# Tokens as the stationary side in the value projections and the second feed-forward product, x turned to rows once, last norm and store row by row

## The reference

```python
def memory_attention(q, mem_n, w_mk, w_mv):
    k = (mem_n @ w_mk).reshape(b_, -1, MEM_HEADS, MEM_HEAD_DIM)
    v = (mem_n @ w_mv).reshape(b_, -1, MEM_HEADS, MEM_HEAD_DIM)
    ...
# second block: 8 retention heads, query and key 256 wide, value and gate 512 wide
scores = jnp.einsum('bhncd,bhnmd->bhncm', qc, kc) * decay_intra[None, :, None]
o_intra = jnp.einsum('bhncm,bhnmv->bhncv', scores, vc)
...
o = head_norm(o, gn_gain, center=True) * jax.nn.silu(g.astype(F32))

def squared_relu_mlp(h, w_up, w_down):
    return jnp.square(jax.nn.relu(h @ w_up)) @ w_down      # 2048 -> 8192 -> 2048
...
        x = x + squared_relu_mlp(rmsnorm(x, norm2[layer]), mlp_w_up[layer], mlp_w_down[layer])
    return rmsnorm(x, final_norm)
```

## Time and profile before

| | us |
|---|---|
| median of 3 runs | 2787.62 (2781.04 to 2793.1) |
| the profiled execution's own time | 2788.26 |
| its span | 2786.7 |
| PE busy | 2718.5 (98%) |
| DVE busy | 1966.6 (71%) |
| ACT busy | 1414.5 (51%) |

### The profile page before, as it was taken

How to read it: one execution, slowest core, us unless ns; L and a number is a source line. 1 busy time by engine, 2 the same in 40 slices (tenths; PEclk the granted TensorE clock), 3 DMA queues, 4 the chain that set the end, 5 groups by cost and what they waited for, 6 DMA issues and landing times.

```text
span 2786.7 us, 45672 instructions
## 1 busy us (share of the span) xinstructions
PE 2718.5 (98%) x15610; PEld 2369.4 (85%) x15610; DVE 1966.6 (71%) x3116; ACT 1414.5 (51%) x2220; POOL 35.5 (1%) x56
## 2 busy tenths in 40 slices
PE   6999999999998999999999999999999999999998
PEld 5888888888887788888888888888888888888887
DVE  5566678888777677777777766767777576675775
ACT  5555455555555455556555444555554444444444
POOL 0000000000000011000000000000000000000000
PEclk9999999999999999999999999999999999999999
DMA  5555454443674344466544555455455555555553
GB/s 229 194 193 194 153 198 163 151 163 126 220 247 142 103 144 154 149 191 209 180 169 175 184 192 188 171 181 175 172 187 191 190 186 195 183 194 184 193 189 113
DMA packets 76349, 495.73 MB, mean 178 GB/s; under 512 B 8544, under 2 KB 8672, under 8 KB 23792
## 3 DMA queue, kind: packets, MB, share of 16 engines
q1 hardware_dynamic: 73568, 478.18, 50.1%
q0 software_dynamic: 2000, 13.70, 1.3%
q10 hardware_dynamic: 704, 2.83, 0.3%
HBM read 486.29 MB, written 8.39 MB: 178 GB/s over the span
## 4 chain that ended last, share of the span: by engine, by line
PE 90%; DVE 4%; ACT 2%; issue 1%; DVEq 1%; DMA 1%; ACTq 0%; POOLq 0%
PE pj L1496 56%; PE pj L1499 29%; PE mx L1513 1%; DVE w_lo L753 1%; ACT w_hi L408 1%; PE mx L1849 0%; PE mx L1669 0%; PE mx L1785 0%; ACT half L413 0%; PE mx L1657 0%; PE mx L1786 0%; PE mx L1841 0%; DMA xT<-in_mem 0%; DMA x_spill<-xT 0%; PE mx L1676 0%
## 5 line engine op out<-in xcount | busy, mean ns | idle before, releaser
L1496 PE MATMUL pj<-hs,w_hi 128*128 128x512 f32 x4400 | 1557.6, 398 | 5.9 <-DVE xT L767 4.7
L753 DVE TENSOR_TENSOR w_lo<-raw,w_hi 128x1024 fp32r<-128x1024 f32 x1010 | 1137.3, 1131 | 436.3 <-ACT w_hi L408 417.3
L408 ACT ACTIVATE w_hi<-raw 128x1024 fp32r<-128x1024 f32 x1010 | 982.7, 979 | 619.1 <-PE pj L1496 607.0
L1499 PE MATMUL pj<-hs,w_lo 128*128 128x256 f32 x4400 | 1231.4, 280 | 0.0
L1496 PEld LDWEIGHTS pj<-hs,w_hi 128*128 128x128 f32 x4400 | 825.8, 188 | 195.5 <-DVE xT L767 5.0
L1496 PE MATMUL pj<-ys,w_hi 128*128 128x512 f32 x2496 | 879.0, 397 | 12.1 <-DVE ys L818 4.0
L1499 PEld LDWEIGHTS pj<-hs,w_lo 128*128 128x128 f32 x4400 | 832.1, 189 | 4.2 <-issue 3.3
L1499 PE MATMUL pj<-ys,w_lo 128*128 128x256 f32 x2496 | 700.2, 281 | 0.0
L1496 PEld LDWEIGHTS pj<-ys,w_hi 128*128 128x128 f32 x2496 | 469.8, 188 | 123.4 <-DVE ys L774 4.6
L413 ACT ACTIVATE half<-pj 128x256 f32<-128x256 f32 x491 | 187.5, 382 | 567.6 <-PE pj L1499 556.4
L1499 PEld LDWEIGHTS pj<-ys,w_lo 128*128 128x128 f32 x2496 | 473.2, 190 | 0.0
(11 more groups left out here) (292 smaller groups left out, 1380.5 us busy)
## 6 DMA issues: line engine op xcount, KB each, us to landing
raw<-in_w_up SPq DMA_DIRECT2D x64, 1024.0 KB, 4.8
raw<-in_w_down SPq DMA_DIRECT2D x64, 1024.0 KB, 4.7
raw<-in_w_ssd SPq DMA_DIRECT2D x48, 1024.0 KB, 4.8
raw<-in_w_ret_a SPq DMA_DIRECT2D x48, 1024.0 KB, 4.7
raw<-in_w_ret_b SPq DMA_DIRECT2D x48, 1024.0 KB, 4.8
raw<-in_w_out SPq DMA_DIRECT2D x64, 640.0 KB, 4.0
raw<-in_w_gate SPq DMA_DIRECT2D x32, 1024.0 KB, 4.7
raw<-in_w_mem SPq DMA_DIRECT2D x16, 1024.0 KB, 4.8
```

The lines of the kernel that those rows point to most:

```text
L408: A(w_hi[:, s, 0:b - a, :], raw[:, c.slot(p, 4), a:b, :], ACT.Copy).then_inc(hi_ready, 1)
L753: TT(w_lo[:, s, 0:b - a, :], raw[:, c.slot(p, 4), a:b, :], w_hi[:, s, 0:b - a, :].bitcast(F32), ALU.subtract).then_inc(split_ready, 1)
L1496: ins = mm(pj[:, k], w_hi[:, s + h, u], m, start=opens and t == 0, stop=False)
L1499: ins = mm(pj[:, k, 0:T], w_lo[:, s + h, u], m[:, 0], start=False, stop=closes and t == order[-1])
```

## The change

In the value panels (`j` 4 to 7 of `mem`, `ret_a`, `ret_b`) and in all panels of `down`, a panel now holds 4 input tiles by 512 output columns instead of 16 by 128. `row_panel` takes 128 tokens of one input tile as the stationary side and moves 512 weight columns: hi tokens with `w_hi`, hi tokens with `w_lo`, lo tokens with `w_hi`. Four panels accumulate in both `pj` banks, one bank for each 128 tokens (`r`), and the result stands token-first. The 512 columns are read as four pieces of 128. SP loads these panels in four pieces of 2 KB a partition.

For `mem` and retention, ACT copies the two banks out (`rows_out`), and the transposes are gone. For `down`, DVE adds each bank to `rows`, to which the residual was turned once during `up0` (32 transposes, 8 groups of 4, and 8 ACT copies). The last norm works on rows: the gain row comes by a transfer, squares are summed row by row, and each 128x512 piece is scaled and stored by itself (8 stores of 256 KB). In retention the product of scores and values moves from behind the tenth panel (`j` = 9) into the ninth (`j` = 8, after 12 of 16 tiles), and most of the gating (`gated(0, 3)`) moves one panel ahead of the end.

```diff
+            def row_panel(name, i, j, src, out_, opens, closes, last=False):
+                c, O = panels(name, i), outputs(name, i)
+                s = 2 * c.slot(j, 2)
+                if opens or last:
+                    order = [(r, u) for r in range(2) for u in range(4)]
+                else:
+                    order = [(r, u) for h in range(2) for r in range(2) for u in (2 * h, 2 * h + 1)]
+                pe.wait_ge(split_ready, c.half(j, 0))
+                for n, (r, u) in enumerate(order):
+                    if n == (2 if opens or last else 4):
+                        pe.wait_ge(split_ready, c.half(j, 1))
+                    if opens and u == 0:
+                        pe.wait_ge(evacuated, O(out_ + r, 1))
+                    bank = pj[:, O.slot(out_ + r, NB)]
...
+                    ins = mm(bank, x_hi, hi, start=opens and u == 0, stop=False)
+                    if n in (0, 6 if opens or last else 4):
+                        ins.then_inc(half_started, 1)
+                    mm(bank, x_hi, lo, start=False, stop=False)
+                    ins = mm(bank, x_lo, hi, start=False, stop=closes and u == 3)
+                    if closes and u == 3:
+                        ins.then_inc(output_ready, 1)
...
+            def rows_out(name, i, r, dst, scale=1.0, sums=None):
+                O = outputs(name, i)
+                act.wait_ge(output_ready, O(4 + r, 1))
+                A(dst, pj[:, O.slot(4 + r, NB)], ACT.Copy, scale=scale, accum_out=sums).then_inc(half_copied, 1)
+                act.drain().then_inc(evacuated, 1)
...
-                        if 5 <= j <= 8:
...
-                            for k in range(2):
-                                ins = transpose_to(mx[:, 1 + n % 2, 128 * k:128 * k + 128],
-                                                   vt_r[:, T * (n % 2) + 128 * k:T * (n % 2) + 128 * k + 128])
...
-                residual(f"down{b}", 1)
+                def down_body(i):
+                    name = f"down{b}"
+                    O = outputs(name, i)
+                    for j in range(4):
+                        split(name, i, j, 0)
+                        if j == 3:
...
+                            for r in range(2):
+                                dve.wait_ge(output_ready, O(r, 1))
+                                w = rows[:, r, bass.ds(i * 512, 512)]
+                                ins = TT(w, w, pj[:, O.slot(r, NB)], ALU.add)
+                                ins.then_inc(evacuated, 1)
+                                if name == LAST:
+                                    dve.drain().then_inc(S["fin_add"], 1)
+                                if name == LAST and isinstance(i, int):
+                                    fin_norm(r)
+                        split(name, i, j, 1)
...
+                    def turn(r):
+                        def four():
+                            if i:
+                                pe.wait_ge(S["rows_copied"], i * 2 + r - 1)
+                            for u in range(4):
+                                ins = transpose_to(mx[:, 2 + r, 128 * u:128 * u + 128],
+                                                   xT[:, i * 4 + u, 128 * r:128 * r + 128])
+                            ins.then_inc(S["rows_turned"], 1)
+                        return four
```

More of the change, by code:

```diff
@@ L159, in carve @@
             return views
-        outs_per = {"gate_out": 8, "out0": 4, "out1": 4, "ret_out_a": 4, "ret_out_b": 4, "mla": 10}
+        outs_per = {f"down{b}": 2 for b in range(FF_BLOCKS)} | {"mem": 6, "ret_a": 10, "ret_b": 10} | {"gate_out": 8, "out0": 4, "out1": 4, "ret_out_a": 4, "ret_out_b": 4, "mla": 10}
         first_panel, first_out = {}, {}
@@ L192, in part, with by_rows, weights @@
             return c, j + AHEAD, 2 * c.slot(j + AHEAD, 2) + h, k if h else 0, max(n, k + 1) if h else min(n, k)
+        def by_rows(name, j):
+            return name.startswith("down") or (name in ("mem", "ret_a", "ret_b") and 4 <= j < 8)
+        def weights(name, i, j, c, p, s, h, a, b):
+            last = name == "ret_out_b" and isinstance(i, int) and i == PHASES[name][1] - 1 and j >= len(PHASES[name][0])
+            if name.startswith("up") or by_rows(name, j) or last:
+                return [raw[:, c.slot(p, 4)].rearrange("p (t k) c -> p t (k c)", t=4)[:, :, 256 * h:256 * h + 256]] + [
+                    w[:, s].rearrange("p (t k) c -> p t (k c)", t=4) for w in (w_hi, w_lo)]
+            return raw[:, c.slot(p, 4), a:b, :], w_hi[:, s, 0:b - a, :], w_lo[:, s, 0:b - a, :]
         def cut(j, n):
@@ L228, in run @@
             n = PHASES[name][1]
-            last = n - 1 if name == ORDER[-1] else n
+            last = n - 1 if name in (ORDER[-1], "ret_out_b") else n
             if last - first == 1:
@@ L355, in _ @@
             run(pool, "mem", spill)
+            pool.wait_ge(S["tables"], 48)
+            with nc.allow_non_contiguous_dma(reason="one row of 2048 gains"):
+                pool.dma_start(gain_spill.rearrange("a (c p) -> p (a c)", p=P), vec[:, VEC["final_2"][0]:VEC["final_2"][1]]
+                               ).then_inc(S["gain_saved"], 16)
             pool.wait_ge(S["x_tile"], 16)
@@ L733, in _ @@
                 run(act, f"up{b}", up_body, int(b == 0))
-                residual(f"down{b}", 1)
-            rsqrt(NORM["b_out"] + 1, nv[:, 0:2], ny[:, 0:2])
-            act.wait_ge(S["fin_scale"], 1)
-            for g in range(1, 8, 2):
-                act.wait_ge(S["fin_rows"], g + 1)
-                A(rows[:, g // 4, 512 * (g % 4):512 * (g % 4) + 512], fin_bank(g), ACT.Copy,
-                  scale=rstd[:, 256 + g // 4:257 + g // 4]).then_inc(S["fin_act"], 1)
+                run(act, f"down{b}", down_body)
         @block.vector
@@ L1862, in _, with up_panel @@
                 residual("ret_out" + ph[3:], 1, ys, {}, 2)
+            def up_panel(name, i, j, before={}, mid={}):
+                c, O = panels(name, i), outputs(name, i)
+                s, k = 2 * c.slot(j, 2), O.slot(j, NB)
+                pe.wait_ge(split_ready, c.half(j, 0))
+                pe.wait_ge(evacuated, O(j, 1))
+                order = [4 * t + 2 * h + u for h in range(2) for t in range(4) for u in range(2)]
+                for n, t in enumerate(order):
+                    h, u = n // 8, n % 8
+                    if n == 8:
+                        pe.wait_ge(split_ready, c.half(j, 1))
+                    if n in mid:
+                        mid[n]()
+                    if n in before:
+                        pe.wait_ge(*before[n])
+                    ins = mm(pj[:, k], w_hi[:, s + h, u], hs[:, t], start=n == 0, stop=False)
+                    if u == 0:
+                        ins.then_inc(half_started, 1)
+                    ins = mm(pj[:, k, 0:T], w_lo[:, s + h, u], hs[:, t, 0], start=False, stop=n == 15)
+                ins.then_inc(output_ready, 1)
@@ L1889, in _tiles @@
+                run(pe, f"down{b}", down_body)
 def _tiles(w, rows, cols):
```

290 lines of the change are left out of this document (167 added, 123 removed).

## The result

The changed kernel is slower: a median of 2797.17 us of 15 runs (2793.44 to 2802.61) against 2789.26 of 15 runs of the kernel before (2776.89 to 2793.1). The ratio is 1.0033, 95% interval 1.0025 to 1.0041. I had forecast 2777 and a range of 2762 to 2791.

A forecast was written before the change was run, and what follows sets the result against it. PE was taken as the bound, busy 2718.5 of 2786.7 us. Terms -11.1 - 10.6 + 3.5 + 11.4 + 2.4 - 1.6 - 4.5 = -10.5 us gave 2777 us against the median 2787.62; range 2762 to 2791.

The forecast's parts named there:

- PE's wait for `y_ret`: After retention: DVE's last three steps shrink from four tiles to one, so PE's 0.8 us wait goes, twice: -1.6 us.
- the tail: Behind the last matmul: norm by rows and smaller stores shorten 14.3 us to 9.8, -4.5 us (-2 to -6).
- Row panels: 104 panels of `down`, retention and `mem`: 24 matmuls at 226.7 ns, 0.107 us less a panel, -11.1 us.
- the panels gain nothing: Rival: matmul time goes with columns, 231.1 ns a step, 11.1 us less gain, 2788 us; chance 0.16.
- a cut moving operand: Rival: reading the moving 512 columns in four pieces costs 13.3 ns for each of 2496 matmuls, 2811 us; chance 0.10.
- weight loads bound the pairs: Rival: each load sets the pace, so row panels fall to 215 ns a matmul, 40 us less, 2737; chance 0.10.
- Transposes gone, and those of `up0`: Transposes removed from retention (7.0 us) and `mem` (3.6), together -10.6 us; 32 new ones in `up0`, +3.5 us.
- The bank in `down`: Behind 15 output groups PE waits 0.76 us for DVE's addition, queued behind a split, to empty bank 0: +11.4 us.
- the bank is free in time: Rival: bank 0 in `down` is emptied before PE needs it, no wait, 2766 us; chance 0.12.
- Scores times values: Retention: the product, moved into the ninth panel, waits 0.3 us for centred values in 8 heads, +2.4 us (0 to 5).
- its norm through by +1.5: Tail: bank 0 is done half a panel earlier, its norm finished 1.5 us after the matmuls end.
- Edits at nothing: Untouched phases: steps between PE's starts taken as unchanged, at no cost; a shift there was named as a sign of error.

## Why the prediction was wrong

The sum came out at -10.5 and the traces give +9.6. **The step that failed is the one that held the steps between PE's starts at 346.7 ns in code that the change does not touch: 9.1 of the 20.1 us.** Behind it come PE's wait for `y_ret` (2.4), retention (2.1), the tail (1.8) and unchanged stages (3.8). By the prediction's own steps:

- **Row panels, 226.7 ns a step: right.** 16 panels of `down` take 87.05 us without waits, 5.44 each. The rivals "the panels gain nothing" (231.1) and "a cut moving operand" (240) have fallen, and so has "weight loads bound the pairs", whose steps would have been 215 ns.
- **Transposes gone, and those of `up0`: right** (-4.5 in `mem`, +3.5 in `up0`).
- **The bank in `down`: right.** 0.76 predicted, 0.78 in the timeline, 12.0 us by its removal against 11.4. The rival "the bank is free in time" has fallen. The step was right, but the result is that this wait eats more than all row panels of the kernel give.
- **Scores times values: right in kind, small in size**, 0.43 us a head instead of 0.3, 1.0 us in all. The terms that the prediction prints (8.8, 0.24 and 0.88) add up to 9.92, not 9.85; with them it would have been 0.42.
- **The rest of retention, 1.1 us: two things at nothing.** In the second head PE waits 0.6 us for DVE's evacuation of a bank (L827): 909 ns lie between two starts that would be 120 apart, 0.8 us, in one head only. And the first ten steps of row panels are longer than 226.7 ns, by some 0.04 us at each of 16 entries, an estimate of 0.6 us from the starts.
- **PE's wait for `y_ret` goes, -1.6: it went, but a longer one took its place.** Before, PE was 0.80 us late. After, it stands at the beginning of `ret_out_a`'s second output for its bank, which DVE has not emptied (timeline of the kernel after):

```profile
1593.32 0.96 DVE L834 TENSOR_TENSOR ys<-kv,ys 128x768 f32 x1 [0.17 <-issue]
...
1594.19 1.22 DVE L814 TENSOR_TENSOR w_lo<-raw,w_hi 128x1024 fp32r<-128x1024 f32 x1
...
1595.33 0.42 DVE L825 TENSOR_TENSOR gen<-pj,half 128x256 f32<-128x256 f32 x1
1595.82 0.43 DVE L827 TENSOR_TENSOR gen<-gen,wdt 128x256 f32<-128x256 f32 x1
...
1596.30 0.50 PE L1730 MATMUL pj<-ys,w_hi 128*128 128x512 f32 x1 [1.39 <-DVE gen L827]
```

  The gating of three tiles, moved a panel earlier (`gated(0, 3)`, its last step is L834), stands ahead of the last gate tile's evacuation (L825, L827), and PE, whose last matmul had started at 1594.64, stands idle for 1.39 us. `ret_out_b` has the same wait, 1.0 us. I had asked who waits for the shortened steps, and not what is queued behind the moved ones.
- **The tail: mechanism right, -2.7 instead of -4.5.** The step that failed is "its norm through by +1.5". The square of the first row waited until the panel's end for ACT's bookkeeping (`output_ready` of the second bank), which I had not followed through ACT's stream. So bank 1's addition ended at 2789.90, 4.2 us behind the matmuls and not 2.2. Without that wait the tail is 10.3 us, near the 9.8 of the sum. The starting point was low as well: of five traces that end in the old code, the one that I read has a tail of 14.5 us and the others 15.5 to 15.7, against which the new 12.4 is 3.1 to 3.3 less.
- **Edits at nothing: wrong, and this is the decisive step.** "The steps between starts" of phases that the change does not touch were held to be fixed at 346.7 ns a pair. That figure comes from `up1` and `down1` of one trace, and holds there for one of two cadences; in the same trace `out0`, `out1` and `ret_out_b` ran at the other. In the changed kernel `gate` and `up1` to `up3` have the slow one, 3.4 and 5.1 us, and `up0`, with its eight new interruptions, too, 1.5 us: 10.0 us, of which 9.1 remain when all stages are taken together. Part of it is luck of the two traces of the kernel before: `gate` was quick in both, but slow in two other traces of the same code. The prediction named this as something that would make it wrong, but gave it no price and no chance.
- **Other stages, +3.8 us.** `ssd` (+1.0) and `latent` to `mla` (+2.4) are unchanged code. Over the 14 traces `latent` to `mla` without the cadence ranges from 377.8 to 382.0 us for code that is as before up to there, and from 379.3 to 383.7 where `mem` has row panels. The granted clock tells most of them apart: from 880 to 955 us, inside these stages, it is 0.93 on average in six of the traces and 0.89 in eight, with stretches at 1.2 GHz of 10 and of 17 us in all, too short for the page's 40 slices. Between a fixed matmul of `out0` and one of `out1`, without the cadence, lie 482.1 to 483.3 us at 0.93 and 486.2 at 0.89 in code as before, and 483.4 to 484.9 and 485.7 to 487.8 where `mem` has row panels. Of the four traces in the table the first of the kernel before and both of the changed one have 0.89, so some 1.5 of the 2.4 us are this (an estimate, half the distance of the two groups). The prediction had "at the upper clock throughout". What the change has to do with it is open, since 0.89 came up in 1 trace of 4 without those row panels and in 7 of 10 with them; so is the rest.

Two things were not told apart. What in PE makes the two cadences, and what decides at a restart, no trace shows: stops of the same 1.39 us drew both. And the slow `up1` to `up3` of the changed kernel itself, 9 of 9 in three traces, come behind a stop (the bank wait), where other stops draw the quick one in 6 of 10; I can say that they are slow, not why always. What the change did there is plain all the same: it cut one run of 4067 matmuls, which one restart decided, and `up1`, `up2` and `up3` are now entered anew, each behind row panels.

## What to carry to other kernels

When the bound engine runs at a steady step, look through the whole trace for the second value of that step before you multiply by it: what a change does to the way into a stage can be worth as much as what it removes. A gain of 0.1 us a panel is spent by a single wait of 0.8 us every fourth panel at twice its size, so follow each consumer's instruction stream to what stands ahead of the instruction that frees a buffer; moving one line here was worth 13.5 us. Where work is moved forward to end one wait, look at what then queues behind it.

## What the runs showed of the hardware

- Alternating float32r matmuls of 512 and 256 columns at 2.4 GHz (granted clock 1.00) run at 346.7 or 353.3 ns a pair, kept from one interruption of PE to the next, over as many as 4067 matmuls at the first value and 1024 at the second.
- Entered from 512-column matmuls at 226.7 ns without a pause, they were slow in 108 of 108 stretches; behind an interruption quick in 1029 of 1762. Many of these are the same places in each of 14 traces; the same stop of 1.39 us gave 12 quick and 19 slow blocks within one execution.
- The 512-column steps have one value, 226.7 ns, behind each kind of entry, once they have settled within some ten steps of up to 241 ns. They read the moving side in four pieces of 128 columns, and are no longer than the 225 to 230 ns of one piece.
- One transpose of a 128x128 block between the two kinds takes 0.1 us (the step around it is 26 + 314 ns instead of 227) and turned 1.7 us around in a phase of 512 matmuls.
- In `latent` to `mla`, where PE has gaps (busy 61 to 66 of 75 us), the granted clock went to 1.2 GHz for 10 us in some executions and 17 in others, and the stage took 2.5 to 3.6 us longer in the latter.
